# Eight of twelve first up-tiles of a convolutional FFN as seven-product quads, with the token combinations on GpSimd

## What is computed

```python
for l in range(DEPTH):                       # 2 layers
    h = _rmsnorm(x, g_mix[l])
    ...                                      # gMLP heads and gated linear attention -> mixed
    x = x + mixed @ w_out[l]                 # output projection, 8 tiles of 128 channels
    h = _rmsnorm(x, g_ffn[l])
    z = _dwconv_centred(h @ w_up[l], conv_w[l], conv_b[l])     # 2 x 2816 channels
    z_gate, z_val = jnp.split(z, [D_FF], axis=-1)
    x = x + (jax.nn.silu(z_gate) * z_val) @ w_down[l]
```

## Time and profile before

| | us |
|---|---|
| median of 3 runs (lowest, highest) | 1083.91 (1083.64, 1084.34) |
| the profiled execution, its own time | 1084.41 |
| span of its instructions | 1082.6 |
| PE busy in the span | 1071.1 |
| POOL, DVE, ACT busy | 636.1, 596.6, 557.4 |

### The profile page before, as it was taken

One profiled execution on the slowest core, in us unless ns is written; L12 is line 12 of the kernel. 1 busy time (PEld: TensorE's weight loads), 2 busy tenths in 40 slices (PEclk: granted clock), 3 DMA queues, 4 the chain that ended last, 5 costly groups with the idle time before them and its releaser, 6 DMA issues.

```text
span 1082.6 us, 18370 instructions
## 1 busy us (share of the span) xinstructions
PE 1071.1 (99%) x6492; PEld 941.5 (87%) x6492; DVE 596.6 (55%) x922; ACT 557.4 (51%) x772; POOL 636.1 (59%) x314
## 2 busy tenths in 40 slices
PE   9999999999999999999999999999999999999997
PEld 7788888888899989998878888888879998899987
DVE  4735755677146730676636359556741776136664
ACT  7835334545266623675548344445444675257651
POOL 5333334344799948995634333434458995789940
PEclk9999999999999999999999999999999999999999
DMA  8232123232999459972522221322349973898512
GB/s 306 96 97 79 59 65 110 78 112 83 247 232 241 119 158 248 208 167 96 173 81 89 79 79 60 97 97 78 101 141 266 231 177 98 241 207 221 133 56 79
DMA packets 45156, 151.12 MB, mean 140 GB/s; under 512 B 5264, under 2 KB 8080, under 8 KB 45072
## 3 DMA queue, kind: packets, MB, share of 16 engines
q1 hardware_dynamic: 35152, 115.42, 32.9%
q0 software_dynamic: 9216, 33.56, 16.9%
q10 hardware_dynamic: 704, 1.07, 0.3%
HBM read 131.15 MB, written 2.10 MB: 123 GB/s over the span
## 4 chain that ended last, share of the span: by engine, by line
PE 70%; POOL 9%; DVE 9%; DMA 4%; ACT 3%; issue 3%; DVEq 0%; ACTq 0%; SPq 0%; POOLq 0%
PE acc L1482 12%; PE acc L1483 12%; PE acc L1484 12%; POOL w_lo L464 8%; PE acc L1796 7%; PE acc L1799 7%; PE acc L1798 7%; DVE arena L1304 3%; PE acc L1608 3%; PE acc L1610 3%; PE acc L1609 3%; DMA mixer_sb<-w_raw 2%; DMA w_raw<-slabs 2%; ACT arena L805 2%; DVE sides L1295 1%
## 5 line engine op out<-in xcount | busy, mean ns | idle before, releaser
L474 POOL TENSOR_TENSOR w_lo<-w_raw,w_hi 128x1024 fp32r<-128x1024 f32 x108 | 262.2, 2448 | 331.8 <-ACT w_hi L541 329.0
L464 POOL TENSOR_TENSOR w_lo<-w_raw,w_hi 128x1024 fp32r<-128x1024 f32 x72 | 190.7, 2752 | 37.4 <-ACT w_hi L824 24.7
L1482 PE MATMUL acc<-feat_hi,w_hi 128*128 128x512 f32 (+1 forms) x496 | 190.1, 383 | 1.6 <-DVE x L1246 1.5
L1483 PE MATMUL acc<-feat_lo,w_hi 128*128 128x512 f32 (+1 forms) x496 | 189.7, 382 | 0.0
L1484 PE MATMUL acc<-feat_hi,w_lo 128*128 128x512 f32 (+1 forms) x496 | 189.6, 382 | 0.0
L541 ACT ACTIVATE w_hi<-w_raw 128x1024 fp32r<-128x1024 f32 x102 | 107.9, 1063 | 139.8 <-PE acc L1484 103.4
L1798 PE MATMUL acc<-xg_lo,w_hi 128*128 128x256 f32 x512 | 144.9, 283 | 0.0
L1799 PE MATMUL acc<-xg_hi,w_lo 128*128 128x256 f32 x512 | 144.9, 283 | 0.0
L1796 PE MATMUL acc<-xg_hi,w_hi 128*128 128x256 f32 x512 | 144.9, 283 | 0.0
L1482 PE MATMUL acc<-xg_hi,w_hi 128*128 128x512 f32 x352 | 139.6, 397 | 0.0
L1483 PE MATMUL acc<-xg_lo,w_hi 128*128 128x512 f32 x352 | 137.1, 389 | 0.0
(11 more groups left out here) (179 smaller groups left out, 2136.6 us busy)
## 6 DMA issues: line engine op xcount, KB each, us to landing
w_raw<-slabs SPq DMA_DIRECT2D x166, 512.0 KB, 3.5
mixer_sb<-slabs SPq DMA_DIRECT2D x16, 512.0 KB, 5.6
w_raw<-slabs POOLq DMA_DIRECT2D x16, 512.0 KB, 6.7
arena<-slabs SPq DMA_DIRECT2D x16, 512.0 KB, 4.9
arena<-slabs POOLq DMA_DIRECT2D x16, 512.0 KB, 7.1
second_s<-slabs SPq DMA_DIRECT2D x8, 512.0 KB, 6.5
mixer_sb<-w_raw POOLq DMA_DIRECT2D x8, 512.0 KB, 8.8
w_raw<-mixer_sb POOLq DMA_DIRECT2D x8, 512.0 KB, 6.6
```

The lines of the kernel that those rows point to most:

```text
L464: pool.tensor_tensor(w_lo[:, w], source, w_hi[:, w].bitcast(F32), ALU.subtract).then_inc(lo_done, 1)
L474: pool.tensor_tensor(w_lo[:, w], w_raw[:, w], w_hi[:, w].bitcast(F32), ALU.subtract).then_inc(lo_done, 1)
L1482: pe.matmul(out, wh, ah, start=first, stop=False)
L1483: pe.matmul(out, wh, al, start=False, stop=False)
```

## The change

Four of the twelve first up-tiles stay plain (`first_ups`); the other eight become two more quads by seven products (quads 0 and 1; the former eight are now 2 to 9). PE therefore needs T1 to T4 right after four up-tiles, so the combinations move into the output projection: ACT scales both x tiles of a pair (`scale_pair`, two copies of 128x512), and POOL makes T1 to T4 from them (`combine`, now four subtractions or additions of 128x256 on POOL instead of DVE, between its low parts). `t_high` and `t_low` move there too. T1's split lies in a buffer of its own at first and is copied by ACT to its old place after quad 1. The slots of the ring for the first ups shift by two (`SKIPPED`), and quads 0 and 1 use the two sets of weight buffers in swapped order (`parity`). The first down projection keeps its 6 blocks and 8 tiles, but is now made like the others: tiles 0 to 2 together, then two blocks of tile 3, then the last two features' blocks.

```diff
+N_QUADS = N_FFN + RING
+N_PARTS = N_QUADS + FIRST_QUADS * UNITS + KT
...
+        t_raw, pair_raw = slot(2, 2)[:, 0:3 * H], slot(20, 2)
...
+            def load_first_part(L):
+
+                load_slab(L, SLABS_FFN // RING, 0)
+                load_a21(L, 0)
+                load_a11(L, 0)
+                load_s2(L, 0)
+                load_a12(L, 0)
+                for j in range(1, RING):
+                    load_slab(L, SLABS_FFN // RING, j)
+                low_of(L, N_FFN + 1)
+                load_a21(L, 1)
+                low_of(L, N_FFN)
+                load_a11(L, 1)
+                low_of(L, N_FFN + 2)
+                load_a12(L, 1)
+                low_of(L, N_FFN + 3)
+                load_a22(L, 0)
+                sp.wait_ge(t1_ready, L + 1)
+                load_s2(L, 1)
+                low_of(L, quad_unit(0) + A22_)
+                load_a22(L, 1)
+                low_of(L, quad_unit(1) + S2_)
+                load_down(L, 0, 1)
+                low_of(L, quad_unit(1) + A22_)
+                load_down(L, 0, 3)
+                low_of(L, quad_unit(1) + S3_)
+                load_down(L, 0, 0)
+                low_of(L, quad_unit(1) + S4_)
+                load_down(L, 0, 2)
+
+            def load_part_slabs(L, d):
+                first, last = PART_QUADS[d][0], PART_QUADS[d][-1]
...
+            def combine(L, k):
+
+                b11, b12, b21, b22 = (pair_raw[:, i * H:(i + 1) * H] for i in range(4))
+                t1, t2 = t1_raw[:, k * H:(k + 1) * H], t_raw[:, 0:H]
+                pool.wait_ge(pair_scaled, 2 * (L * KP + k + 1))
+                if L * KP + k:
+                    pool.wait_ge(t_ready, L * KP + k)
+                pool.tensor_tensor(t1, b11, b12, ALU.subtract).then_inc(t1_raw_done, 1)
+                pool.wait_ge(t1_raw_done, L * KP + (k + 1))
+                pool.tensor_tensor(t2, b22, t1, ALU.add).then_inc(t2_done, 1)
+                pool.wait_ge(t2_done, L * KP + (k + 1))
+                pool.tensor_tensor(t_raw[:, H:2 * H], b11, t2, ALU.subtract)
+                pool.tensor_tensor(t_raw[:, 2 * H:3 * H], b21, t2, ALU.subtract).then_inc(t_raw_done, 1)
+
...
-                low_slabs(at + (RING if L == 0 else 0), at + N_DOWN + RING)
-                for p in range(FULL_PARTS):
-                    n = at + first_unit(p)
+                low_slabs(at + (RING if L == 0 else 0), at + SLABS_FFN - RING)
+                for j in range(RING):
+                    low(at + SLABS_FFN - RING + j, raw(j), 1 + SKIPPED if j == RING - 1 else 1)
+                    if j % 2:
+                        combine(L, j // 2)
+                combine(L, 2)
+                for d in range(LAST + 1):
+                    first, last = PART_QUADS[d][0], PART_QUADS[d][-1]
+                    n = at + quad_unit(first)
                     low(n - 4, raw(0))
+                    if d == 0:
+                        add_s1(L, first)
                     low(n - 3, raw(1))
+                    if d == 0:
+                        combine(L, 3)
                     low(n - 2, raw(2))
-                    add_s1(L, p, 0)
+                    if d > 0:
+                        add_s1(L, first)
+                    else:
+                        add_s2(L, first)
                     low(n - 1, raw(3))
-                    add_s2(L, p, 0)
-                    for s in range(KP):
-                        low_quad(L, p, s)
-                    down = at + first_unit(p, KP)
+                    if d > 0:
+                        add_s2(L, first)
+                    for q in PART_QUADS[d]:
+                        low_quad(L, q, q < last)
...
+                for m in range(RING):
+                    act.wait_ge(acc_ready, L * NU + (N_OUT + m + 1))
+                    act.wait_ge(raw_loaded[m], 16 * (L * LOADS) + 16 * (SLABS_FFN // RING))
+                    split_hi(m, 1 + SKIPPED if m == RING - 1 else 1)
+                    out_tile(m)
+                    if m % 2:
+                        scale_pair(m // 2)
+                    elif m:
+                        t_high(m // 2 - 1)
+                out_tile(4)
+                t_high(1)
+                out_tile(5)
+                scale_pair(2)
+                first_high(0)
+                out_tile(6)
+                t_high(2)
+                first_high(1)
+                out_tile(7)
+                scale_pair(3)
+                first_high(2)
+                first_high(3)
+                root("ffn_spread", stdT_done, L * NSIDE + NSIDE, rstdT[:, :], 1.0 / D, S)
+                t_high(3)
+                act.activation(t1_hi, t1_raw, ACT.Copy).then_inc(t1_hi_done, 1)
+                first_quad()
+                for d in range(LAST + 1):
+                    if d > 0:
+                        first_highs(d)
+                    for q in PART_QUADS[d]:
+                        quad_step(d, q)
+                    last_step(d)
+                    if d == 0:
+                        for to, of in ((xg12_hi, t1_hi), (xg12_lo, t1_lo)):
+                            act.activation(to, of.rearrange("p (k s) -> p k s", k=KP), ACT.Copy).then_inc(t1_moved, 1)
...
-                            act.wait_ge(raw_loaded[j], 16 * (L * LOADS) + 4 * slab + 32)
-                            split_hi(j)
+                            (high_s1, high_a11, high_a12, high_s2)[j](0)
...
+                    first_scale(0)
+                    first_taps(0)
+                    t1_low()
+                    t_low(KP - 1)
+                    first_scale(1)
+                    first_taps(1)
+                    first_gate(0)
+                    first_scale(2)
+                    feat_low(0, 0, 0)
+                    first_taps(2)
+                    first_scale(3)
+                    first_taps(3)
+                    first_gate(1)
...
+                    early = blocks - 2
+                    order = [(k, j) for j in range(3) for k in range(early)]
+                    if d == 0:
+                        order += [(k, 3) for k in range(2)]
+                    order += [(k, j) for k in range(early, blocks) for j in range(3)]
+                    order += [(k, 3) for k in range(2 if d == 0 else 0, blocks)]
...
+                first_ups()
+                for d in range(LAST + 1):
+                    for q in PART_QUADS[d]:
+                        up_products(d, q)
+                    down_products(d, KT if d < LAST or L < DEPTH - 1 else TAIL[0])```

Two places in the queues, each before and now. On POOL, in the output projection of the first layer, before the change: after the output tiles' low parts (the loop) only low parts of slabs follow, and the first transfer that adds slabs.

```order
L474 TENSOR_TENSOR w_lo<-w_raw,w_hi 128x1024 [waits hi_done]
L470 REGISTER_ALU
L470 COMPARE_AND_BRANCH
L464 TENSOR_TENSOR w_lo<-w_raw,w_hi 128x1024 [waits hi_done] x3
L480 DMA w_raw<-slabs 128x1024 [waits a21_loaded0]
L464 TENSOR_TENSOR w_lo<-w_raw,w_hi 128x1024 [waits hi_done]
L488 DMA mixer_sb<-w_raw 128x1024 [waits s1_added0,s2_loaded0]
```

More of the change, by code:

```diff
@@ L289, in encoder @@
         NX = 4 * KT
-        NY = 2 * FIRST_TILES
+        NY = RING
         def on_its_own(eng):
@@ L1744, in _ @@
                         turn(3)
-                with pe.Fori(0, KT // RING) as q:
+                for q in range(KT // RING):
                     for j in (1, 2, 3):
```

763 lines of the change are left out of this document (365 added, 398 removed).

## The result

The changed kernel takes 1094.11 us (median of 4 runs, 1092.47 to 1097.7) against 1083.97: ratio 1.0098, 95% interval 1.0073 to 1.0123. It is slower, 3 us more than the forecast of 1091 and inside its range. Its profiled execution took 1092.47 with a span of 1090.3, 7.7 more than the span before. Run again beside the experiments it took 1095.8 (1.0109, 1.0095 to 1.0124).

The account below looks back on a forecast made before the run. PE, busy 99% of the span, was taken as the bound. Per layer, 8.3 us of new waits against 4.6 removed add 3.7, 7.4 in two, to 1084.41; less 0.5 for the median, 1091 us, range 1082.5 to 1098.

Parts of the forecast that it names:

- Removed: PE's matmul time in two quads (3.2 us) and the x wait (1.43) go: 4.6 us per layer, 9.3 in two.
- The wait for x: First down projection: PE's 1.43 us per layer above pitch, waiting for x that DVE adds late, goes.
- Wait 1: First up-tile: its low part stands on POOL behind pair 2's combination; PE waits 2.7 us (0.9 to 4.1).
- Wait 2: Quad 0's fourth product: PE waits 1.8 us (1.5 to 3.9) for ACT's copies, partly earlier, before quad 0.
- Wait 3: First down projection: 14 blocks, not 18, cover the last two features' low parts; PE waits 1.4 us.
- Wait 4: Quad 2 and behind: chain of low part, load, S1, S2 comes 2.8 us later; 2.4 us taken.
- The sum: Whole kernel: 8.3 us of waits per layer against 4.6 removed, 3.7 more per layer, 7.4 in two.
- (d): From quad 0 on, POOL becomes the bound: waits of 12 us and more per layer, about 1100; chance 0.07.
- (a): Faster: POOL's 256 pieces cheap, holds miss, S2's chain at its median; waits 2.5 to 4.0 us per layer; chance 0.12.

Follow-up runs that it names:

- the fastest kernel: Changed kernel with low parts, copies, a feature, cover blocks and quad 2's early slabs reordered, plus T1's copies and S2's transfer moved later: 1077.57 us (0.9935).

## Why the prediction was right, and where it was not

**Removed.** The saving on PE by pitch held: quads 0 and 1 without a wait take 40.31, two plain quads 43.52, 3.2 less. The wait for x went too, but it was smaller than I had read it: of the 1.43 above the pitch 0.98 stood at x and 0.34 further ahead, at 262.71, where the kernel before with early slabs waits for DVE's low part of a feature.

**Wait 1** was taken at 2.7 and is 1.7: POOL's pieces cost 0.74 and met one hold, and they began at 185.22, not at 185.6 or later. But the step that failed is deeper: I added it as a term of its own, and counted DVE's scaling as 10.8 us behind PE's first up-tile. In the changed kernel it was 10.95 (202.11 - 191.16), which looks right, but only because PE's own wait had moved its start: with the wait removed, tile 0's scaling started at 201.67, 12.1 behind PE, and quad 0 no earlier. DVE's queue runs by itself, with 2.8 and 1.7 us of holds in it.

**Wait 2** (1.8) was 1.88 and 1.69, with its first part before quad 0, as said. **Wait 3** (1.4) was 1.50 and 1.76. Both have the mechanism forecast, a queue in order. Neither can be had back alone, which the forecast did not say.

**Wait 4** (2.4) was 2.05 in the first layer and 3.63 in the second, counting the gap before quad 2. The chain was the one forecast: the transfer for S1 went out at 281.10 against 277.95, 2.5 later counted from the down projection's start, where I had 2.8. That it is a chain of transfers and not POOL's pace, which I left at "POOL's pace binds in all four quads", is the half that was wrong: with the slabs early the same POOL keeps up.

**The sum** came out for the profile, 7.4 forecast and 7.8 measured, and in part by luck. I had 3.7 for each layer; it was 3.04 and 4.74. Where I had 8.3 us of waits per layer there were 7.1 and 8.8, and where I had 4.6 removed it was about 4.1 and 4.0.

The median is 10.1 above before, more than the profile's difference, because the profiled execution was the fastest of the four. The second profile of the same kernel (1094.52) shows what varies: its waits for the features were 0.34 and 0.48 longer, and the one before quad 2 in the second layer 1.37 longer. There GpSimd issued the transfers for S1 and S2 at 816.79 and 824.60, 7.8 apart, since S1 landed late; in the first profile it was 816.11 and 822.23, 6.1 apart. These waits make up most of the 2.05 between the two profiled times. My price of wait 4 took such a chain from one profile.

A second term may come on top: after some long waits of PE its clock was lower. In three experiments the profile shows it (2.27 us idle, then 0.52 for 3.4; 4.90, then 0.50 for 6.0; 5.89, then 0.73 for 6.3). But 2.51 idle for x in the run with the combinations on VectorE left 1.00 behind it, as did up to 2.08 in the two profiles of the changed kernel, so the length of the wait alone does not decide. The four runs of the changed kernel have mean clocks of 0.998, 0.999, 0.998 and 0.995, and the last is the one of 1097.7, 3 us or more above the others; 0.003 of 1095 is 3.3 us. That such a dip sits behind the wait for the features in that run is likely, not shown. The Trainium skill's page "TensorE: Matmul & The Clock Gate" (section "What's actually happening") says that an idle array falls to the lower clock until it has worked again; the three dips agree with it, each behind an idle stretch and gone while PE worked.

**The rivals.** (d), GpSimd as the bound, is excluded by the runs with early slabs. Of (a), the cheap pieces on GpSimd came true, and it was not enough. In the fastest kernel the stretch from the output projection to quad 5 is 4.2 and 3.3 us shorter per layer than before. Of this, 2.35 and 1.38 are the old waits in the quads, which the early slabs took away; the other 1.8 and 1.9 are what stays of the 4.6 removed. Against the kernel before with early slabs, which has lost the old waits as well, it is 4.8 us faster, of 6.4 us less work on PE. That is what two more quads by seven are worth between these two orders. 1.6 of the 4.8 is that the other kernel waits longer for the fifth slab's low part (1.94 and 1.82 against 1.07 and 1.08), and its order was not tuned in other respects.

The prediction held against the change that GpSimd's combinations would meet more of VectorE's work. The run with the combinations on VectorE speaks against that: its operations were held just as much there.

## What to carry to other kernels

Waits of one engine that stand a few microseconds apart are often one queue seen at several places: price each as if the others were there, and test by removing all of them, since one removed alone came back here at the next place. A queue's start is read from what its own engine did, not from where the waiting engine stood. Where a chain of transfers stands behind a low part, look for a buffer that comes free earlier before you move any arithmetic; it gave 9.4 us alone, where none of four other moves gave more than 1.6. And a transfer that waits for another must not stand ahead of work that is due.

## What the runs showed of the hardware

- A VectorE operation can be held by more than one GpSimd instruction: 6.04 us for a work of 1.22, across two low parts back to back (2.67 and 2.65). The Trainium skill's page "SBUF — State Buffer" (section "SBUF: two separate sides") has the other engine blocked for one whole instruction; here it was two in a row.
- 256 columns at the full clock take 0.1200 us and 512 take 0.2267: 0.1067 more for 256 columns more (2.4 GHz), and 0.013 for each matmul on top. At half clock 256 columns took 0.213 (1.2 GHz), with nothing on top. Two quads by seven are 336 matmuls of 256 columns where 168 of 512 would be the same arithmetic; the 168 x 0.0133 = 2.2 us on top are why one eighth less arithmetic gave 3.2 us and not 5.4.
- Moving an operation by less than 1 us against the other engine changed its length almost fivefold, through that hold. T1's low part, at the same place in DVE's order, took 6.04 where it began 0.1 us behind POOL's low part, and 1.28 in the fastest kernel, where it began 0.75 ahead of it:

```profile
202.46 1.28 DVE L1426 TENSOR_TENSOR feat_lo<-mixer_sb,feat_hi 128x1024 fp32r<-128x1024 f32 x1
...
203.21 2.81 POOL L570 TENSOR_TENSOR w_lo<-w_raw,w_hi 128x1024 fp32r<-128x1024 f32 x1
```
